# Odd-layer attention scores: fp32 matmuls replaced by three short-form passes over a high part and a remainder

## The reference

```
q = rms_norm(proj[..., :w].reshape(bsz, seq, N_HEADS_C, HEAD_DIM), c_q_gain)
k = rms_norm(proj[..., w:2 * w].reshape(bsz, seq, N_HEADS_C, HEAD_DIM), c_k_gain)
s = jnp.einsum("bqhd,bshd->bhqs", qb, k).astype(jnp.float32) * scale
s = s + jnp.transpose(cq, (0, 2, 1))[..., None] - c_k[:, :, None, :]
s = jnp.where((key_pos[None, :] <= t[:, None])[None, None], s, -jnp.inf)
p = jax.nn.softmax(s, axis=-1)
```

## Time and profile before

| | us |
|---|---|
| median of 3 runs | 936.95 |
| lowest and highest run | 936.66, 938.24 |
| profiled execution | 938.5 |
| its span | 936.7 |
| TensorE busy in the span | 927.2 |
| DVE busy | 627.6 |
| ACT busy | 561.5 |
| odd layer, about | 290 to 410 |

### The profile page before, as it was taken

The page is one execution under the profiler, slowest core; times in us unless marked ns, Lnnn a source line. Parts: engine busy times, 40 slices in busy tenths (PEclk is TensorE's granted clock), DMA queues, the critical chain, the costliest instruction groups (busy, mean ns, idle before and its releaser), DMA issues.

```text
span 936.7 us, 14128 instructions
## 1 busy us (share of the span) xinstructions
PE 927.2 (99%) x5608; PEld 788.2 (84%) x5608; DVE 627.6 (67%) x1137; ACT 561.5 (60%) x927; POOL 98.4 (11%) x142
## 2 busy tenths in 40 slices
PE   9999999999999999999999999999999999999997
PEld 7876888888888877788888888999988889988876
DVE  6767687764446565678776454677479757677885
ACT  6697565553435787665554343656487547778774
POOL 0210000000000000000000017255003100311101
PEclk9999999999999999999999999999999999999999
DMA  9733565565554435236555555234433545421201
GB/s 365 315 138 124 180 225 180 181 210 193 180 186 174 153 117 180 89 137 221 184 180 188 209 213 193 92 135 139 137 136 115 229 161 180 180 92 45 92 23 46
DMA packets 22418, 152.59 MB, mean 163 GB/s; under 512 B 2513, under 2 KB 2769, under 8 KB 4945
## 3 DMA queue, kind: packets, MB, share of 16 engines
q1 hardware_dynamic: 21424, 148.25, 43.9%
q0 software_dynamic: 640, 3.15, 1.0%
q10 hardware_dynamic: 288, 0.30, 0.1%
HBM read 150.64 MB, written 1.05 MB: 162 GB/s over the span
## 4 chain that ended last, share of the span: by engine, by line
PE 91%; ACT 3%; DVE 3%; issue 1%; DMA 1%; SPq 0%; ACTq 0%; DVEq 0%
PE bank L189 19%; PE bank L191 19%; PE bank L190 19%; PE bank L1165 13%; PE bank L1166 6%; PE bank L931 1%; PE bank L2323 1%; PE bank L2347 1%; PE bank L2332 1%; PE bank L955 1%; PE bank L944 1%; PE bank L1609 1%; DVE w_hi_lo L159 1%; PE bank L761 1%; PE bank L1594 1%
## 5 line engine op out<-in xcount | busy, mean ns | idle before, releaser
L159 DVE TENSOR_TENSOR w_hi_lo<-raw,w_hi_lo 128x2048 fp32r<-128x2048 f32 x121 | 277.3, 2295 | 135.9 <-ACT w_hi_lo L155 135.8
L155 ACT ACTIVATE w_hi_lo<-raw 128x2048 fp32r<-128x2048 f32 x135 | 257.8, 1913 | 107.6 <-PE bank L191 106.4
L1165 PE MATMUL bank<-h,w_hi_lo 128*128 128x512 f32 x512 | 179.5, 397 | 0.0
L1166 PE MATMUL bank<-h,w_hi_lo 128*128 128x256 f32 x512 | 143.1, 280 | 0.0
L189 PE MATMUL bank<-h,w_hi_lo 128*128 128x256 f32 x448 | 129.3, 289 | 0.2 <-DVE ml_x L1871 0.2
L190 PE MATMUL bank<-h,w_hi_lo 128*128 128x256 f32 x448 | 124.9, 279 | 0.0
L191 PE MATMUL bank<-h,w_hi_lo 128*128 128x256 f32 x448 | 124.9, 279 | 0.0
L1165 PEld LDWEIGHTS bank<-h,w_hi_lo 128*128 128x128 f32 x512 | 96.2, 188 | 23.1 <-issue 0.2
L189 PE MATMUL bank<-w_hi_lo,mlp_u_hi 128*128 128x512 f32 x256 | 100.0, 390 | 0.0
L191 PE MATMUL bank<-w_hi_lo,mlp_u_lo 128*128 128x512 f32 x256 | 99.7, 390 | 0.0
L190 PE MATMUL bank<-w_hi_lo,mlp_u_hi 128*128 128x512 f32 x256 | 99.7, 390 | 0.0
(11 more groups left out here) (402 smaller groups left out, 1585.3 us busy)
## 6 DMA issues: line engine op xcount, KB each, us to landing
raw<-in_chunks SPq DMA_DIRECT2D x136, 1024.0 KB, 4.8
even_bias<-in_even POOLq DMA_DIRECT2D x8, 384.0 KB, 3.4
xres<-in_x SPq DMA_DIRECT2D x2, 512.0 KB, 5.5
raw<-in_chunks SPq DMA_DIRECT2D x2, 512.0 KB, 6.4
ml_z<-in_ml SPq DMA_DIRECT2D x1, 896.0 KB, 5.9
small<-in_small SPq DMA_DIRECT2D x1, 559.5 KB, 11.7
final_gain<-in_fnorm SPq DMA_DIRECT2D x1, 512.0 KB, 3.4
out<-final_xn SPq DMA_DIRECT2D x1, 512.0 KB, 2.6
```

What stands on the lines that cost most here:

```text
L155: act.activation(w_hi[slot][:, :], raw[slot][:, :], ACT.Copy).then_inc(hi_ready, 1)
L159: dve.tensor_tensor(w_lo[slot][:, :], raw[slot][:, :], w_hi[slot][:, :].bitcast(F32), ALU.subtract).then_inc(lo_ready, 1)
L1165: pe.matmul(dst[:, :], w_hi[slot][:, cols], h[:, k, :, :], start=(k == 0), stop=False)
L1166: last = pe.matmul(dst[:, 0:S], w_lo[slot][:, cols], h[:, k, 0, :], start=False, stop=(k == KT - 1))
```

## The change

`q_odd` and `k_odd` become fp32r, so ACT's `keep` writes a rounded high part. A new step `keep_low` on DVE reads the same PSUM banks again, multiplies with the gain, subtracts the high part and writes the remainder: two operations on 128x512, four times (first k half, first q half, second k half, second q half). It waits for `kept` and raises `low_kept`. TensorE's four waits for `kept` of q and k become waits for `low_kept`. `score` hands over to a new `score_short` where a pair has remainders: for each tile three fp32r passes for each head, q by k, q by k's remainder, q's remainder by k, and then the decay terms as before. Per pair and head that is 3 + 1 matmuls for each tile, in place of one fp32 matmul (two records) and one. The remainders lie in memory that is free at the time: the upper four tiles of `oy_lo` and `oy_hi`, the lower four of `q_odd`, and a new tensor behind the odd layer's working set. The even layer keeps its fp32 scores.

```diff
@@ -832,7 +832,7 @@
     class HeadNorm:
 
 
-        def __init__(self, stack, name, stats, halves=0, kept=0):
+        def __init__(self, stack, name, stats, halves=0, kept=0, lows=0):
             self.stats = stats
             self.sq = sb(stack, f"{name}_sq", [P, TT, WIDE])
             self.xs = [sb(stack, f"{name}_xs{i}", [P, TT, WIDE]) for i in range(2)]
@@ -842,6 +842,7 @@
                 Count("head_sq", 4 * TT), Count("head_ss", 4 * TT), Count("head_std", 4 * TT))
             self.rstd_ready, self.xs_ready = Count("head_rstd", 4), Count("head_xs", 4)
             self.x_turned, self.kept = Count("head_turned", 8), Count("head_kept", kept)
+            self.low_kept = Count("ns_wg", lows)
 
         def square(self, act, n, t, src):
             w = src.shape[1]
@@ -898,6 +899,14 @@
                 last = act.activation(dst[:, 2 * i:2 * i + 2, :].rearrange("p a s -> p (a s)"), bank[banks[i]][:, :],
                                       ACT.Copy, scale=gain)
             last.then_inc(self.kept.sem, 1)
+
+        def keep_low(self, dve, kept, banks, gain, high, low):
+            dve.wait_ge(self.kept.sem, self.kept.at(kept))
+            for i in range(2):
+                last = dve.scalar_tensor_tensor(low[:, 2 * i:2 * i + 2, :].rearrange("p a s -> p (a s)"), bank[banks[i]][:, :], gain,
+                                                high[:, 2 * i:2 * i + 2, :].rearrange("p a s -> p (a s)").bitcast(F32),
+                                                ALU.mult, ALU.subtract)
+            last.then_inc(self.low_kept.sem, 1)
 
     class Attention:
 
@@ -924,6 +933,8 @@
             at_bank = self.banks_of[i % 2]
             if i >= 2:
                 pe.wait_ge(self.y_lo_done.sem, self.y_lo_done.at(i - 1))
+            if b["k_low"] is not None:
+                return self.score_short(pe, i)
             for t in range(TT):
                 rows = b["key_rows"]
                 for e in range(2):
@@ -936,6 +947,21 @@
                                      rows[e][1][:, 0:self.KEYS[t]], start=False, stop=True)
             last.then_inc(self.scores.sem, 1)
 
+        def score_short(self, pe, i):
+
+            b = self.pairs[i]
+            rows = b["key_rows"]
+            for t in range(TT):
+                n, q = self.KEYS[t], slice(t * P, (t + 1) * P)
+                dst = [bank[at][:, self.PS[t]:self.PS[t] + n] for at in self.banks_of[i % 2]]
+                for a, w in (("q", "k"), ("q", "k_low"), ("q_low", "k")):
+                    for e in range(2):
+                        last = pe.matmul(dst[e], b[a][HALVES[e], q], b[w][HALVES[e], 0:n], start=(a, w) == ("q", "k"),
+                                         stop=rows is None and a == "q_low")
+                for e in range(2 if rows is not None else 0):
+                    last = pe.matmul(dst[e], rows[e][0], rows[e][1][:, 0:n], start=False, stop=True)
+            last.then_inc(self.scores.sem, 1)
+
         def turn(self, pe, i):
             pe.wait_ge(self.scaled.sem, self.scaled.at(4 * (i + 1)))
             for e in range(2):
@@ -1024,7 +1050,7 @@
                               self.y_hi[:, tile, :].bitcast(F32), ALU.subtract).then_inc(self.y_lo_done.sem, 1)
 
     def pair(**kw):
-        base = dict(key_rows=None, sinks=None, bias_loaded=None)
+        base = dict(q_low=None, k_low=None, key_rows=None, sinks=None, bias_loaded=None)
         base.update(kw)
         return base
 
@@ -1397,8 +1423,8 @@
             pe.matmul(self.bank[:, n:2 * n], upper, a[:, 1, :], start=False, stop=True).then_inc(self.sums.sem, 1)
 
     os_ = ExitStack()
-    q_odd = sb(os_, "odd_q", [P, 8, S])
-    k_odd = sb(os_, "odd_k", [P, 8, S])
+    q_odd = sb(os_, "odd_q", [P, 8, S], F32R)
+    k_odd = sb(os_, "odd_k", [P, 8, S], F32R)
     ov = sb(os_, "odd_v", [P, TT, D])
     oqg = sb(os_, "odd_qg", [P, 1])
     sb(os_, "pad_odd_y", [P, 56])
@@ -1416,7 +1442,14 @@
         sem("nlog2_cleared"), sem("nlog2_ready"), sem("decay_done"), sem("decay_kept"), sem("pick_ready"))
     wf_split, oqg_ready = sem("wf_split"), sem("odd_qg_ready")
     f_done, f_kept, f_turned, f_scaled = sem("f_done"), sem("f_kept"), sem("f_turned"), sem("f_scaled")
+    ODD_WORK = 7312
+    with ExitStack() as tmp:
+        sb(tmp, "odd_below", [P, ODD_WORK])
+        k_low_last = sb(tmp, "odd_k_low", [P, 4, S], F32R)
+    q_low = [oy_lo[:, 4:8, :], q_odd[:, 0:4, :]]
+    k_low = [oy_hi[:, 4:8, :], k_low_last]
     pairs = [pair(tile=i, q=q_odd[:, i, :], k=k_odd[:, i, :], mask=[causal, causal],
+                  q_low=q_low[i // 4][:, i % 4, :], k_low=k_low[i // 4][:, i % 4, :],
                   v=[[ov[:, t, n * DH:(n + 1) * DH] for t in range(TT)] for n in (2 * i, 2 * i + 1)],
                   key_rows=[(pick[HALVES[e], 2 * i + e:2 * i + e + 1].to_broadcast([DH, P]), decay[HALVES[e], :]) for e in range(2)])
              for i in range(8)]
@@ -1424,7 +1457,7 @@
     m1_turned = Turned("m1in", sm("g_mlp1"), (0, 1, 2, 3), h)
     o_sq = sb(os_, "odd_x2", [P, TT, WIDE])
     oo_stats.scratch = [o_sq[:, t, :] for t in range(TT)]
-    o_norm = HeadNorm(os_, "on", mlp0.stats)
+    o_norm = HeadNorm(os_, "on", mlp0.stats, lows=4)
     o_att = Attention(os_, "oat", pairs, oy_hi, oy_lo, (2, 3), (0, 1))
     o_out = OutPhase("oout", O_OUT, (4, 5, 6, 7), range(8), o_att, m1_turned, oo_stats)
     os_.close()
@@ -3128,7 +3161,7 @@
                                     ident[0:HEADS, 0:HEADS])
             last.then_inc(f_turned, 1)
             in_chunk(pe, O_IN + 3, 1, (6, 7), o_norm)
-            pe.wait_ge(o_norm.kept.sem, o_norm.kept.at(1))
+            pe.wait_ge(o_norm.low_kept.sem, o_norm.low_kept.at(1))
             in_chunk(pe, O_IN + 4, 0, (4, 5), o_norm)
             o_norm.turn(pe, 1, (6, 7))
             pe.wait_ge(nlog2_ready, 1)
@@ -3137,7 +3170,7 @@
             pe.matmul(bank[1][:, P:S], rows_of[0], ones, start=True, stop=False)
             pe.matmul(bank[1][:, P:S], rows_of[1], upper, start=False, stop=True).then_inc(decay_done, 1)
             in_chunk(pe, O_IN + 5, 1, (4, 5), o_norm)
-            pe.wait_ge(o_norm.kept.sem, o_norm.kept.at(2))
+            pe.wait_ge(o_norm.low_kept.sem, o_norm.low_kept.at(2))
             pe.wait_ge(pick_ready, 1)
             pe.wait_ge(decay_kept, 2)
             o_att.score(pe, 0)
@@ -3160,12 +3193,12 @@
             o_att.score(pe, 3)
             in_half(pe, O_IN + 9, 1, 1, 5).then_inc(chunk_used, 1)
             o_att.values(pe, 2)
-            pe.wait_ge(o_norm.kept.sem, o_norm.kept.at(4))
+            pe.wait_ge(o_norm.low_kept.sem, o_norm.low_kept.at(3))
             in_chunk(pe, O_IN + 10, 0, (6, 7), o_norm)
             o_norm.turn(pe, 3, (4, 5))
             in_chunk(pe, O_IN + 11, 1, (6, 7), o_norm)
             o_att.turn(pe, 3)
-            pe.wait_ge(o_norm.kept.sem, o_norm.kept.at(5))
+            pe.wait_ge(o_norm.low_kept.sem, o_norm.low_kept.at(4))
             o_att.score(pe, 4)
             o_out.pe(pe, o_norm.kept, 5)
 
@@ -3412,6 +3445,7 @@
                 last = dve.scalar_tensor_tensor(forget.f[:, t, :], bank[1][:, P + t * HEADS:P + (t + 1) * HEADS],
                                                 mlp0.stats.factor(t), sm("b_forget"), ALU.mult, ALU.add)
             last.then_inc(forget.ready.sem, 1)
+            o_norm.keep_low(dve, 1, (4, 5), sm("c_k_gain"), k_odd[:, 0:4, :], k_low[0])
             rest_for(dve, O_IN + 3)
             o_norm.reduce(dve, 1, 8)
             o_norm.scale(dve, 1, [bank[6][:, :], bank[7][:, :]])
@@ -3426,6 +3460,7 @@
             for low in (slice(ROWS, 2 * ROWS), slice(3 * ROWS, P)):
                 last = dve.tensor_tensor(decay[low, :], bank[1][low, 0:S], decay[low, :].bitcast(F32), ALU.subtract)
             last.then_inc(decay_kept, 1)
+            o_norm.keep_low(dve, 2, (6, 7), oqg[:, 0:1], q_odd[:, 0:4, :], q_low[0])
             rest_for(dve, O_IN + 5)
             o_att.mask(dve, 0)
             o_att.scale(dve, 0)
@@ -3440,6 +3475,7 @@
             o_att.scale(dve, 2)
             rest_for(dve, O_IN + 8)
             o_att.low(dve, 1)
+            o_norm.keep_low(dve, 4, (6, 7), sm("c_k_gain"), k_odd[:, 4:8, :], k_low[1])
             rest_for(dve, O_IN + 9)
             o_att.mask(dve, 3)
             o_att.scale(dve, 3)
@@ -3447,6 +3483,7 @@
             o_norm.scale(dve, 3, [bank[4][:, :], bank[5][:, :]])
             o_att.low(dve, 2)
             rest_for(dve, O_IN + 10)
+            o_norm.keep_low(dve, 5, (4, 5), oqg[:, 0:1], q_odd[:, 4:8, :], q_low[1])
             rest_for(dve, O_IN + 11)
             o_out.dve(dve, [[], [(O_OUT, 0)], [(O_OUT, 1)], [(O_OUT + 1, 0)]], [(O_OUT + 1, 1)])
```

## The result

The changed kernel takes 938.86 us in the median of 21 runs (936.92 to 940.3), the kernel before 936.89 us in 21 runs beside it (936.51 to 939.19). The ratio is 1.0019, with a 95% interval of 1.0013 to 1.0025. So it is a little slower, by 0.19%: under the 0.2% taken as the bound, and clear of zero. The forecast was 937.2 us, within 935.4 to 939.0. One of the 12 runs of `low_only` further down took 1147.45 us at a granted clock of 0.75, where all others here had full clock, and counts in no comparison.

A forecast was written before the change was run, and what follows sets the result against it. TensorE's queue was taken as the bound: eight score blocks at +0.025 us give +0.2 us, the DVE work nothing, so 936.95 + 0.2 = 937.2 us; own range 936.4 to 938.2, whole range 935.4 to 939.0.

The forecast's parts named there:

- What bounds the kernel: Whole program: TensorE's queue sets the time, busy 927.2 of 936.7 us; one 0.3 us wait in the odd layer.
- The score block: Odd-layer scores on TensorE: +0.11 us first tile, -0.085 us second, +0.025 us a pair, +0.2 us for the layer.
- The first rival: Score block: no weight load shows, only passes count; 1.5 us won, 935.4 us; chance 0.10.
- the four-pass rule: Skill page: true fp32 takes four passes, so three would save a quarter of the streaming, some 1.3 us.
- The DVE work: Four `keep_low` steps in the odd layer, 1.4 us each, 5.6 us in all, each fitting without delaying TensorE.
- The second rival: Inside `score_short`: the two halves take turns streaming, +0.5 us a pair, +4.0 us, 941.1 us; chance 0.07.
- The third rival: DVE in the odd layer: `keep_low` costs twice as much, 3 us each; 1.2 us in all, 938.2 us; chance 0.05.
- The time: Whole program: median 936.95 + 0.2 = 937.2 us, no change within 0.2%; that outcome was given 0.83.
- the forecast's own range: Whole program time: 936.4 to 938.2 us, from run spread, drift of a pass and the DVE bound; chance 0.78.
- The layer's +0.2: Odd layer on TensorE: eight score blocks each 0.025 us longer, +0.2 us in all.
- I carry the difference over to the median: Last step: the +0.2 us, summed inside the profiled span of 936.7 us, is added to the median of 936.95 us.

The follow-up runs named there:

- low_only: Only the DVE part, against the kernel before: rounded q and k, `keep_low` and its waits, scores as fp32 matmuls of the high parts; 938.34 us, ratio 1.0008.
- two_pass: The changed kernel without the third pass (q's remainder by k) in all eight pairs; ran once, 935.07 us, in no comparison.

## Why the prediction was right, and where not

*What bounds the kernel*: right. TensorE's queue sets the time, and its only wait in the layer stayed, 0.2 us where it was 0.3.

*The score block*: right, to 0.01 us. 0.11 us a load in the first tile, 0.115 us a pass in the second, 1.11 us for the block where the sum gave 1.09 + 0.025. `two_pass` shows the cause, the load that no short stream hides. The first rival (no load shows, 0.90 us) and the second (halves in turn, 1.6 us) are both out by the 1.11 us of the block; the four-pass rule goes with the first rival. (The second rival's time was added up wrongly: 936.95 + 4.0 is 941.0 us, not 941.1.)

*The DVE work*: right. 1.40 us a step against 1.4; the first ends at 309.27 and the second at 324.15 where TensorE wants it at 325.17, 1.0 us of room. The third makes the mask of pair 3 start at 354.99 instead of 354.04, and with the 0.27 us by which the whole layer starts later taken off, that is 0.7 us late against TensorE's queue (0.8 was forecast), and the norm's tile is ready at 361.22 + 1.29 = 362.51 for 363.81, 1.3 us ahead. `low_only` costs nothing in either group. The third rival, `keep_low` at twice the price, is out.

*The time*: right within the range, but by luck. 938.86 us lies under the upper end of 939.0, which was set for a `keep_low` of twice its price plus half the spread of three runs, and above the 938.2 at which the forecast's own range ended. The layer's +0.2 came out as +0.17 us in the trace and as 0.15 to 0.4 us between runs of the same rhythm, but the median moved by 2 us, and I had no term for the rest. The step that failed is the last one, "I carry the difference over to the median". The profiled execution of before was 1.5 us over the median, and the runs shown were 936.66, 936.95 and 938.24. I took that for what lies around a span. It was the sign of two levels, and the profile was of the upper one; that is why the two profiles differ by 0.5 us and the medians by 2. I also took the 527 us behind the layer, from 410 us on, as fixed, without a term in the sum. Their instructions didn't change; the rhythm of 87 us of them did, in most runs, and that is 1.6 us of the 2.

Of the 0.5 us between the two spans, 0.3 is there by 16 us, at the start: the eight transposes of the first half of `x` took 1.06 us in the profile of before and 1.73 in that of after. They took 1.84 us in the second profile of the unchanged kernel, so the change isn't the cause. The kernel before:

```profile
5.58 1.06 PE L761 MATMUL bank<-small,xres 128*128 128x128 f32 x8 [0.25 <-DMA xres<-in_x]
```

The changed kernel:

```profile
5.65 1.73 PE L761 MATMUL bank<-small,xres 128*128 128x128 f32 x8
```

And of the kernel before, profiled again:

```profile
5.65 1.84 PE L761 MATMUL bank<-small,xres 128*128 128x128 f32 x8
```

What stays open: why eight transposes exchange the two rhythms and one more pass keeps them, and how longer score blocks, 22 to 85 us ahead of the restart, come to start the phase in the short rhythm and so to leave it in the long one in 42 runs of 43. That they do it is read from the shares of runs; the mechanism is not shown. That the kernel before was in the long one in 14 of 35 runs in one session and in 18 of 21 in another, on another chip, says that something besides the program has a part in it.

## What to carry to other kernels

For a matmul with few moving columns, count weight loads, not columns: three short passes of 128 columns cost more than one fp32 matmul (0.33 against 0.22 us here), with 256 columns they cost less (0.35 against 0.43 us), and sizes between weren't tried. When the runs of an unchanged kernel lie at two levels, find out by the spans which one a profile is of before comparing it with anything, and compare a change within a level. A change of 0.2% that no row explains may be the share of runs in a rhythm and not its own work; an idle pass of 64 columns next to the suspected place is a cheap test of it, though no cure: by the traces it leads from either rhythm to the other.

## What the runs showed of the hardware

A stream of alternating passes of 512 and 256 columns with nothing to wait for can run in two stable rhythms, 1.04 and 1.06 us for three steps, and keeps the one it restarts in for 86 to 87 us. In the second MLP eight transposes in the middle of the stream exchange the two (11 traces of 11), and with one pass of 64 columns behind them the rhythm stays (3 of 3); in the first MLP the short one follows whatever ran ahead. With that pass the changed kernel was in the long one in 3 of 11 runs, without it, in other sessions, in 42 of 43. Passes on 64 rows each, of the two halves, run side by side whether they alternate in the program or come three and three (a block of 1.11 and 1.12 us), and the later half's first pass then starts ahead of the earlier half's second. A weight load of 128 columns takes 0.11 us of the queue and isn't hidden by a short-form pass of 128 columns; short-form passes of 256 columns start 0.115 us apart, and a pass of an fp32 matmul on 256 columns took 0.21 us.
